# A hybrid encoder step on one core: parameter loads and transposes at the head, the last rotation of the convolution, and every second high part of its normed frames moved

## The chip, the cores and the metric

One Trainium2 chip, one of its cores. The metric is the device time of one execution in microseconds (us), the median of three runs. The engines are called PE (TensorE), DVE (VectorE), ACT (ScalarE), POOL (GpSimd) and SP (SyncE, which only issues transfers here).

## The reference

One inference step over 512 prompt frames and 32 sample frames of width 1024, with two layers. Layer 0 has chunk-band attention and gated linear attention side by side, layer 1 a Conformer convolution module. Each is followed by a squared-ReLU MLP of width 4096. The part that the change touches:

```python
def conv_module(xn, buf, w1, b1, w_dw, b_dw, ln_g, ln_b, w2, b2):
    u = xn @ w1 + b1
    u = u[..., :D_MODEL] * jax.nn.sigmoid(u[..., D_MODEL:])
    full = jnp.concatenate([buf.astype(u.dtype), u], axis=1)
    y = lax.conv_general_dilated(full, w_dw.astype(full.dtype)[:, None, :], window_strides=(1,),
                                 padding='VALID', dimension_numbers=('NWC', 'WIO', 'NWC'),
                                 feature_group_count=D_MODEL) + b_dw
    y = jax.nn.silu(layer_norm(y, ln_g, ln_b))
    return y @ w2 + b2, full[:, -(CONV_W - 1):]
```

## The kernel before, in words

All 544 frames stay in SBUF, channels on partitions: `resid` holds 8 tiles of 128 channels x 544 frames. Every weight matrix is streamed in units of 1024 x 256 (1 MB); there are 92. SP loads a unit into one of two buffers `w_raw` (L416) as soon as the buffer's last user has been split. ACT makes its high part (`split_hi`, L608, type fp32r), DVE its low part (`split_lo`, L1514), and PE multiplies: high x high, high weights x low frames, low weights x high frames, 48 products a tile of 128 output channels (`tile`, L1017; `together` L1040 takes both tiles of a unit column by column, `by_halves` L1056 does so for half of the frames at a time). Frames come as a high part `x_h` and a low part `x_l` too. The order of work on each engine is written out by hand and tied by semaphores: an engine executes its list in order and waits where its next instruction needs another's.

The head: SP loads the rows of x, two weight units and then 23 small parameter loads (`load_parameters`, L386). PE transposes x into four rotating slots of PSUM (L996), which DVE copies to `resid` (L1568); ACT and DVE make high and low parts (L637, L1536). PE runs unit 0 (`together`, with the wait `x_ready` per column), then transposes the parameters (`parameters`, L1077 to L1085), then runs unit 1. DVE scales unit 0's result (L1609, which frees its slot in PSUM) and then copies the parameters (L1579 to L1591).

Before long pauses PE runs dummy products (`keep_clock`, L980) on `ones`.

Between the first MLP and the convolution module comes a norm (`norm`, ACT L643 and L676, DVE L1551 and L1557), then ACT's split of the module's second weight unit, then the first gate (sigmoid, L894).

The convolution: 8 column tiles `m`. Unit `m` of `c_w_pw1` gives gate and value; DVE multiplies them into `glu` (L1912). PE does 20 to 24 of the 31 taps as 32 x 32 diagonal products (`taps`, L1398) and needs for them three copies of the tile whose partitions are rotated by 32, 64 and 96, `glu_rot`. POOL makes them: six transfers per column (L579, L580), counted in `moved`. DVE does the rest of the taps (L1929 to L1936) and the sample frames (L1948), then adds PE's sums (L1961, which waits for `taps_done`). After the last column come the layer norm over channels: means by PE (`add_mean`, L1414), DVE subtracts (L1990), ACT squares (L934), PE sums (L1438), ACT takes the root (L927), DVE inverts (L1994).

Then the normed frames, 16 pieces `j` (8 column tiles for the first 288 frames, 8 for the other 256): DVE scales by 1/std (`cv_scaled`, L2001), ACT applies Silu (L944) into one of three tiles `xn`, ACT copies it to `x_h` (L947), DVE subtracts for `x_l` (L2011), and PE multiplies it by the first unit of `c_w_pw2` (`by_halves`, L1056). DVE's list is: low part of `j`, scaling of `j + 2`, and so on, with the low part of the next weight unit behind `j = 3` (L1514).

Of the kernel before, what the change touches and what calls it, by code (L numbers as in the profile page):

```python
# [74 lines left out]
def tile0(u):  # L75


    return 8 + 2 * u
# [6 lines left out]
def hybrid_kernel(nc, x_prompt, x_sample, cache_a_k, cache_a_v, state_b, cache_c, norm_mix_g, norm_ffn_g,  # L85
# [160 lines left out]
    gains_T, gains_ready = sem("gains_T"), sem("gains_ready")  # L246
    r_ready, x_sums, r_rows, r_spread, r_T = (
        sem(n) for n in ("r_ready", "x_sums", "r_rows", "r_spread", "r_T"))

    x_copied = [sem(f"x_copied{n}") for n in range(4)]  # L250
# [129 lines left out]
    def _(sp):  # L380
# [5 lines left out]
        def load_parameters():  # L386
            for at, n, src in ((V_B1, 16, as_rows(c_b_pw1)), (V_BDW, 8, as_rows(c_b_dw)), (V_LNG, 8, as_rows(c_ln_g)),
                               (V_LNB, 8, as_rows(c_ln_b)), (V_B2, 8, as_rows(c_b_pw2)), (V_GB, 2, as_rows(b_gate_b)),
                               (V_ON, 1, b_out_norm_g)):
                sp.dma_start(vec_rows[at:at + n, :], src).then_inc(rows_landed, 16)  # L390
            for at, src in ((V_QG, a_q_norm_g), (V_KG, a_k_norm_g)):
                for b in range(2):
                    sp.dma_start(vec_rows[at:at + 1, b * DA:(b + 1) * DA], src).then_inc(rows_landed, 16)
            sp.dma_start(wlr[:], w_view(w_in_ab[0])[:, :, N_PROJ * P:N_PROJ * P + RANK]).then_inc(rows_landed, 16)
# [7 lines left out]
            sp.dma_start(gate_w[:], b_gate_w_up[0]).then_inc(rows_landed, 16)  # L402
            sp.dma_start(rel, a_rel_bias[0]).then_inc(rows_landed, 16)
            sp.dma_start(state_s[:], state_b[0, 0].rearrange("(a b) k v -> (b k) a v", b=2)).then_inc(rows_landed, 16)
# [30 lines left out]
        stream(U_PW2, 4, columns(c_w_pw2[0]))  # L435
# [13 lines left out]
    def _(pool):  # L449
# [123 lines left out]
        for m in range(KT):  # L573
# [16 lines left out]
    def _(act):  # L590
# [7 lines left out]
        for at, src in ((V_MIX, norm_mix_g), (V_FFN, norm_ffn_g)):  # L598
            act.dma_start(vec_rows[at:at + 16, :], as_rows(src)).then_inc(gains_landed, 16)

# [54 lines left out]
        for k in range(KT):  # L655
            hi_gain(0, x_h, k, V_MIX, x_copied[k % 4], k // 4 + 1)
            if k == 1:
                split_hi(0, 0, 0)
                for late in (6, 7):
                    act.wait_ge(gemm_done, late + 1)  # L660
                    act.activation(resid[:, late, :], flat(late % 4)[:, 0:TOK], ACT.Copy).then_inc(x_copied[late % 4], 1)
# [1417 lines left out]
```

## Time and profile before

| what | value |
|---|---|
| median of 3 runs | 1371.54 us (1370.0 to 1373.36) |
| the profiled execution | 1374.85 us, of which the span of its core 1373.1 us |
| granted clock of PE, mean | 0.993 of full speed |
| PE busy | 1344.9 us (98%) |
| PE weight loads | 1274.7 us (93%), beside the products |
| DVE busy | 703.2 us (51%) |
| ACT busy | 472.7 us (34%) |
| POOL busy | 86.5 us (6%) |
| chain of waits, by engine | PE 90%; DVE 5%; ACT 2%; issue 2%; DMA 1% |
| chain of waits, the line of `tile` | 70% |
| moved by DMA | 119.90 MB, mean 87 GB/s |

The span is the time from the first to the last instruction of the profiled execution, whose own time is a little longer. Busy shares are means over the whole span; what a change in one stage does is read from that stage.

### The profile page before, as it was taken

Reading aid. Unit: us, or ns where it says so; the run is one execution under the profiler, and the core shown is the slowest. Engines: PE = TensorE matmul, PEld = TensorE weight load, DVE = VectorE, ACT = ScalarE, POOL = GpSimd, SP = SyncE. Lnnn points to the kernel's source line nnn. Section 1 sums busy time; section 2 is a strip of 40 time slices with the busy share of each in tenths; the row PEclk is TensorE's granted clock in tenths of the full one; section 3 lists DMA queues with packets and bytes.
Section 4 is the critical chain, followed back from the end, with each engine's and each line's share of the span. In section 5 each row is a group of like instructions: output and inputs, shape, how many; then the busy total and the mean of one; then the engine's idle time right before and its main releaser. Section 6 shows DMA issues by size and latency. Waiting matters only on the chain.

```text
span 1373.1 us, 27650 instructions
## 1 busy us (share of the span) xinstructions
PE 1344.9 (98%) x11649; PEld 1274.7 (93%) x11649; DVE 703.2 (51%) x1028; ACT 472.7 (34%) x792; POOL 86.5 (6%) x145
## 2 busy tenths in 40 slices
PE   8999999999999999999999999989999999999998
PEld 7998888779999999999999888858999999999998
DVE  5693568575544334334324788877544334334322
ACT  4221556434333223123122544445433223223111
POOL 4001100001100000000011111101100000000000
PEclk9999999999999999999999999999999999999999
DMA  7223300222222222222221433302222221222221
GB/s 253 80 92 106 119 27 2 95 72 93 82 83 82 92 92 92 92 85 74 96 84 62 112 110 106 104 16 69 93 93 92 93 92 61 95 90 92 92 78 50
DMA packets 107293, 119.90 MB, mean 87 GB/s; under 512 B 4435, under 2 KB 103358, under 8 KB 106943
## 3 DMA queue, kind: packets, MB, share of 16 engines
q1 hardware_dynamic: 102783, 101.50, 23.1%
q0 software_dynamic: 4352, 17.02, 4.2%
q8 instruction: 72, 1.18, 0.3%
q14 instruction: 22, 0.18, 0.0%
q10 hardware_dynamic: 64, 0.02, 0.0%
HBM read 104.66 MB, written 7.21 MB: 81 GB/s over the span
## 4 chain that ended last, share of the span: by engine, by line
PE 90%; DVE 5%; ACT 2%; issue 2%; DMA 1%; POOL 0%; SPq 0%; DVEq 0%; ACTq 0%; POOLq 0%
PE ps L1017 70%; PE ps L1173 4%; PE ps L1398 3%; PE ps L1040 3%; DVE rstd L1613 2%; PE ps L1190 1%; PE ps L1284 1%; PE ps L980 1%; PE ps L1223 1%; PE ps L1207 1%; PE ps L1056 1%; PE ps L1002 1%; DVE w_l L1514 1%; PE ps L1438 1%; DMA x_rows<-in_x_sample 1%
## 5 line engine op out<-in xcount | busy, mean ns | idle before, releaser
L608 ACT ACTIVATE w_h<-w_raw 128x2048 fp32r<-128x2048 f32 x92 | 175.4, 1907 | 276.4 <-PE ps L1017 272.9
L1514 DVE TENSOR_TENSOR w_l<-w_raw,w_h 128x2048 fp32r<-128x2048 f32 x92 | 210.8, 2291 | 102.8 <-ACT w_h L608 102.7
L1017 PE MATMUL ps<-x_h,w_h 128*128 128x272 f32 x1152 | 242.0, 292 | 2.4 <-ACT sig L894 1.5
L1017 PE MATMUL ps<-x_l,w_h 128*128 128x272 f32 x1152 | 238.6, 288 | 0.0
L1017 PE MATMUL ps<-x_h,w_l 128*128 128x272 f32 x1152 | 238.2, 288 | 0.0
L1017 PE MATMUL ps<-xf_h,w_h 128*128 128x272 f32 x1024 | 212.9, 289 | 0.0
L1017 PE MATMUL ps<-xf_l,w_h 128*128 128x272 f32 x1024 | 211.2, 287 | 0.0
L1017 PE MATMUL ps<-xf_h,w_l 128*128 128x272 f32 x1024 | 210.9, 287 | 0.0
L1017 PEld LDWEIGHTS ps<-x_h,w_h 128*128 128x128 f32 x1152 | 180.9, 189 | 9.1 <-issue 8.7
L1017 PEld LDWEIGHTS ps<-x_l,w_h 128*128 128x128 f32 x1152 | 182.6, 189 | 0.0
L1017 PEld LDWEIGHTS ps<-x_h,w_l 128*128 128x128 f32 x1152 | 180.7, 188 | 0.0
L1017 PEld LDWEIGHTS ps<-xf_l,w_h 128*128 128x128 f32 x1024 | 161.5, 188 | 0.0
L1017 PEld LDWEIGHTS ps<-xf_h,w_h 128*128 128x128 f32 x1024 | 159.9, 188 | 0.2
L1017 PEld LDWEIGHTS ps<-xf_h,w_l 128*128 128x128 f32 x1024 | 159.8, 188 | 0.0
L1861 DVE TENSOR_TENSOR resid<-ps,resid 128x544 f32 x64 | 46.3, 724 | 200.6 <-PE ps L1017 199.7
L870 ACT ACTIVATE relu<-relu 128x544 f32<-128x544 f32 x64 | 42.2, 659 | 239.9 <-DVE relu L1879 239.9
L1017 PE MATMUL ps<-odd_h,w_h 128*128 128x272 f32 x512 | 106.8, 290 | 0.0
L1017 PE MATMUL ps<-odd_l,w_h 128*128 128x272 f32 x512 | 105.6, 287 | 0.0
L1017 PE MATMUL ps<-odd_h,w_l 128*128 128x272 f32 x512 | 105.5, 287 | 0.0
L1879 DVE SCALAR_TENSOR_TENSOR relu<-ps,xn 128x544 f32<-128x544 f32 x64 | 46.2, 722 | 89.6 <-PE ps L1017 89.5
L1017 PEld LDWEIGHTS ps<-odd_l,w_h 128*128 128x128 f32 x512 | 80.8, 188 | 0.0
L1017 PEld LDWEIGHTS ps<-odd_h,w_l 128*128 128x128 f32 x512 | 79.9, 188 | 0.0
(278 smaller groups left out, 1653.5 us busy)
## 6 DMA issues: line engine op xcount, KB each, us to landing
w_raw<-in_w_ffn_up SPq DMA_DIRECT2D x32, 1024.0 KB, 5.3
w_raw<-in_w_ffn_down SPq DMA_DIRECT2D x32, 1024.0 KB, 5.1
w_raw<-in_w_in_ab SPq DMA_DIRECT2D x12, 1024.0 KB, 5.3
w_raw<-in_c_w_pw SPq DMA_DIRECT2D x12, 1024.0 KB, 6.1
w_raw<-in_w_out_ab SPq DMA_DIRECT2D x4, 1024.0 KB, 5.5
glu_rot<-glu POOLq DMA_DIRECT2D x16, 203.2 KB, 5.4
resid_scratch<-resid POOLq DMA_DIRECT2D x1, 2176.0 KB, 8.1
resid<-resid_scratch POOLq DMA_DIRECT2D x1, 2176.0 KB, 9.0
```

Of the source, the lines that this page charges most:

```text
L608: act.activation(w_h[s][:], w_raw[:, s], ACT.Copy).then_inc(w_hi, 1)
L870: act.activation(relu2[:, m, :], relu[:, m, :], ACT.Square).then_inc(relu2_done, 1)
L980: pe.matmul(ps[:, bank, 0:2 * P], any_bits[:, 0:P], any_bits, start=True, stop=True)
L1002: ins = pe.matmul(dst[:, a, :], w[:], src[:, a * n:(a + 1) * n], start=start, stop=stop)
L1017: ins = pe.matmul(ps[:, 2 * m + t, 0:HALF], a[s][:, k, w], b[:, k, t * HALF:(t + 1) * HALF], start=(k == 0 and q == 0), stop=(k == KT - 1 ...
L1040: ins = pe.matmul(ps[:, 2 * m + t, 0:HALF], a[s][:, k, w], b[:, k, t * HALF:(t + 1) * HALF], start=(k == 0 and q == 0), stop=(k == KT - 1 ...
L1173: ins = pe.matmul(ps[:, 2 * m + t, 0:HALF], a[u % 2][:, k, m * P:(m + 1) * P], b[:, k, t * HALF:(t + 1) * HALF], start=(k == 0 and q == 0) ...
L1398: ins = pe.matmul(ps[to, 4 + r, :], diag[rows, s, tap, :], src, start=(n == 0), stop=(n == rounds(m) - 1))
L1514: dve.tensor_tensor(w_l[s][:], w_raw[:, s], w_h[s][:].bitcast(F32), ALU.subtract).then_inc(w_lo, 1)
L1613: dve.reciprocal(rstd[:, 0:TOK], sumsq[:]).then_inc(rstd_ready, 1)
L1861: dve.tensor_tensor(r, slot(m), r, ALU.add).then_inc(slot_free[m], 1)
L1879: dve.scalar_tensor_tensor(out=halves(relu[:, m, :]), in0=slot(m), scalar=0.0, in1=halves(r_tok), op0=ALU.max, op1=ALU.mult).then_inc(slot ...
```

## The change

It moves work, and changes nothing that is computed. (1) Of the parameter loads eleven go from SP's list to ACT's; the eight that PE's transposes need stay on SP, ahead of the second weight unit, and four follow it with a semaphore of their own, `late_rows`. (2) x is transposed into three slots instead of four, PE transposes the parameters ahead of unit 0 and runs eight dummies behind them, and DVE copies the parameters before it scales. (3) ACT splits the second unit of `c_w_pw1` ahead of the second norm. (4) Of the last column's six rotations the three that end at partition 128 go to ACT's queue, counted in `moved_last`; SP holds the third unit of `c_w_pw2` until all six have landed; PE runs eight dummies ahead of the last taps. (5) POOL copies every second `x_h` of the normed frames.

```diff
-    x_copied = [sem(f"x_copied{n}") for n in range(4)]
+    x_copied = [sem(f"x_copied{n}") for n in range(3)]
...
             if first:
                 for s in range(2):
                     sp.dma_start(w_raw[:, s], source(s)).then_inc(w_landed[s], 16)
-                load_parameters()
+                    (load_parameters, load_late_parameters)[s]()
...
-        stream(U_PW2, 4, columns(c_w_pw2[0]))
+        stream(U_PW2, 2, columns(c_w_pw2[0]))
+
+        sp.wait_ge(moved[(KT - 1) % 2], KT // 2 * 96 - 48)
+        sp.wait_ge(moved_last, 48)
+        stream(U_PW2 + 2, 2, columns(c_w_pw2[0], 512))
...
                 pool.dma_start(glu_rot[0:at, m % 2, j - 1, :], glu[P - at:P, m, 0:PAD + SEQ]).then_inc(moved[m % 2], 16)
-                pool.dma_start(glu_rot[at:P, m % 2, j - 1, :], glu[0:P - at, m, 0:PAD + SEQ]).then_inc(moved[m % 2], 16)
+                if m < KT - 1:
+                    pool.dma_start(glu_rot[at:P, m % 2, j - 1, :], glu[0:P - at, m, 0:PAD + SEQ])\
+                        .then_inc(moved[m % 2], 16)
+
+
+        for j in range(1, 2 * KT, 2):
+            c, k = j // KT, j % KT
+            pool.wait_ge(cv_silu, j + 1)
+            pool.tensor_copy(x_h[:, k, cv_span(c)], xn[:, j % 3, cv_span(c)]).then_inc(cv_hi_odd, 1)
...
         ffn(0, U_FFN0, lambda u: phase(u, 4, squares_of(2, u)))
+        split_hi(U_PW1, 0, 1)
         norm(2, X_MIX1)
...
-        split_hi(U_PW1, 0, 1)
...
         split_hi(U_PW2, 0, 1)
+
+        act.wait_ge(slot_free[1], KT - 1 + (tile0(U_PW1) // 2 + 1))
+        act.wait_ge(taps_done, KT)
+        for j in range(1, ROTS):
+            at = P - j * (P // ROTS)
+            act.dma_start(glu_rot[at:P, (KT - 1) % 2, j - 1, :], glu[0:P - at, KT - 1, 0:PAD + SEQ])\
+                .then_inc(moved_last, 16)
         act.activation(no_use[:], eps[:], ACT.Sqrt)
...
-            act.wait_ge(cv_silu, j + 1)
-            act.activation(x_h[:, k, cv_span(c)], xn[:, j % 3, cv_span(c)], ACT.Copy).then_inc(cv_hi, 1)
+            if j % 2 == 0:
+                act.wait_ge(cv_silu, j + 1)
+                act.activation(x_h[:, k, cv_span(c)], xn[:, j % 3, cv_span(c)], ACT.Copy).then_inc(cv_hi, 1)
...
-            pe.wait_ge(rows_landed, 16 * 23)
+            pe.wait_ge(rows_landed, 16 * 19)
...
-        for n in range(4):
-            pe.wait_ge(x_copied[n], 2)
+        parameters()
+        for n in range(2):
+            pe.wait_ge(x_copied[n], 3)
+        keep_clock(8, 0)
         together(0, 0, x_h, x_l, x_ready)
-        parameters()
...
+        pe.wait_ge(slot_free[1], tile0(U_PW2) // 2)
+        keep_clock(8, 2)
         taps(KT - 1)
...
             if u == 0:
+                parameters()
                 dve.wait_ge(r_ready, 1)
...
-            if u == 0:
-                parameters()
...
-            dve.wait_ge(cv_hi, j + 1)
+            dve.wait_ge((cv_hi, cv_hi_odd)[j % 2], j // 2 + 1)
```

PE at the head, from the last transpose of x to the first products of unit 0. Before:

```order
L996 MATMUL ps<-ident,x_rows 128x128 x4
L996 MATMUL ps<-ident,x_rows 128x32
L1040 MATMUL ps<-x_h,w_h 128x272 x2
L1040 MATMUL ps<-x_l,w_h 128x272 x2
L1040 MATMUL ps<-x_h,w_l 128x272 x2
```

Now:

```order
L1021 MATMUL ps<-ident,x_rows 128x128 x4
L1021 MATMUL ps<-ident,x_rows 128x32
L1102 MATMUL ps<-ident,vec_rows 128x85
L1104 MATMUL ps<-ident,dw_rows 128x31 x8
L1107 MATMUL ps<-ident,dw_cross 128x18 x8
L1110 MATMUL ps<-ident,cc_rows 128x30 x8
L1005 MATMUL ps<-ones 128x256 x8
L1065 MATMUL ps<-x_h,w_h 128x272 x2
```

The 25 transposes of parameters and eight dummies have come between the transposes of x and unit 0.

SP's queue at the head, which has to bring those parameters. Now (before, both weight units stood ahead of all small loads):

```order
L387 DMA x_rows<-in_x_sample 32x1024
L408 DMA w_raw<-in_w_in_ab 128x8x256
L390 DMA dw_rows<-in_c_w_dw 31x1024
L394 DMA dw_cross<-in_c_w_dw 6x8x96
L395 DMA dw_cross<-in_c_w_dw 6x8x32
L394 DMA dw_cross<-in_c_w_dw 6x8x64
L395 DMA dw_cross<-in_c_w_dw 6x8x64
L394 DMA dw_cross<-in_c_w_dw 6x8x32
L395 DMA dw_cross<-in_c_w_dw 6x8x96
L396 DMA cc_rows<-in_cache_c 30x1024
L408 DMA w_raw<-in_w_in_ab 128x8x256
L399 DMA wlr<-in_w_in_ab 128x8x16
```

The second weight unit has moved behind eight loads, and four stand behind it.

ACT at the normed frames behind the convolution, the first pieces. Before:

```order
L944 ACTIVATE xn<-cv,vecs 128x288
L947 ACTIVATE x_h<-xn 128x288
L944 ACTIVATE xn<-cv,vecs 128x288
L947 ACTIVATE x_h<-xn 128x288
L944 ACTIVATE xn<-cv,vecs 128x288
L947 ACTIVATE x_h<-xn 128x288
```

Now:

```order
L968 ACTIVATE xn<-cv,vecs 128x288
L972 ACTIVATE x_h<-xn 128x288
L968 ACTIVATE xn<-cv,vecs 128x288 x2
L972 ACTIVATE x_h<-xn 128x288
L968 ACTIVATE xn<-cv,vecs 128x288 x2
L972 ACTIVATE x_h<-xn 128x288
```

Every second copy has left ACT's list; POOL's has eight of them, between its last rotations and the store of the convolution's cache.

## Rows read from the trace of the kernel before

**Rows 1.** timeline of PE, head of the kernel (start us, us, engine, line, operation, idle before)
```profile
18.25 0.61 PE L1040 MATMUL ps<-x_h,w_h 128*128 128x272 f32 x2 [2.28 <-DVE x_l L1536]
...
32.74 0.24 PE L1077 MATMUL ps<-ident,vec_rows 85*128 85x85 f32 x1
...
34.51 0.52 PE L1017 MATMUL ps<-x_h,w_h 128*128 128x272 f32 x2
```
**Rows 2.** busy time and granted clock of one stretch at the head
```profile
18.25:21.90 3.65, 3.65 (x17) 3.65 (x18) 3.33 (x5) 3.62 (x7) 0.00 (x0) 0.53 0.22 69
```
**Rows 3.** timeline of DVE, after the first unit's product
```profile
32.25 1.41 DVE L1609 TENSOR_TENSOR proj<-ps,xn 128x544 f32<-128x544 f32 x2 [4.76 <-PE ps L1040]
```
**Rows 4.** timeline of SP's queue, parameter loads
```profile
3.50 1.21 SPq L410 DMA_DIRECT2D w_raw<-in_w_in_ab  x2
4.74 5.57 SPq L390 DMA_DIRECT2D vec_rows<-in_c_b_pw  x1
...
13.97 0.43 SPq L395 DMA_DIRECT2D dw_rows<-in_c_w_dw  x1
...
19.25 0.46 SPq L401 DMA_DIRECT2D cc_rows<-in_cache_c  x1
```
**Rows 5.** landing times of the first two weight tiles (L410)
```profile
DMA to landing us min/median/max: 9.6/10.8/12.0
```
**Rows 6.** the page's costliest groups: ACT's split (x count, busy, mean ns)
```profile
L608 ACT ACTIVATE w_h<-w_raw 128x2048 fp32r<-128x2048 f32 x92 | 175.4, 1907 | 276.4 <-PE ps L1017 272.9
```
**Rows 7.** timeline of ACT, second norm and first gate
```profile
744.68 0.71 ACT L643 ACTIVATE sumsq<-ps,eps 128x544 f32<-128x544 f32 x1 [2.69 <-PE ps L1002]
...
763.12 1.28 ACT L894 ACT_TABLE_LOAD   x1 [2.01 <-PE ps L1040]
```
**Rows 8.** timeline of PE, end of the convolution
```profile
889.22 4.15 PE L1414 MATMUL ps<-cv,mean_d 128*128 128x288 f32 x16
...
897.45 1.08 PE L1398 MATMUL ps<-glu,diag 32*32 32x512 f32 x4 [4.08 <-DMA glu_rot<-glu]
...
910.68 1.04 PE L980 MATMUL ps<-ones 128*128 128x256 bf16 x8
```
**Rows 9.** timeline of DVE, end of the convolution
```profile
906.35 0.69 DVE L1961 TENSOR_TENSOR rstd<-ps,rstd 128x512 f32<-128x512 f32 x1 [7.04 <-PE ps L1398]
```
**Rows 10.** busy time and granted clock, last column's taps
```profile
897.40:902.30 4.90, 4.85 (x90) 2.17 (x97) 1.84 (x3) 0.00 (x0) 0.00 (x0) 0.50 0.00 0
```
**Rows 11.** timeline of POOL, last rotations
```profile
887.98 0.52 POOL L579 DMA_DIRECT2D glu_rot<-glu  x1 [14.62 <-DVE glu L1912]
```
**Rows 12.** DMA issues of 764 to 777 us (KB each, us to landing)
```profile
glu_rot<-glu POOLq DMA_DIRECT2D x2, 203.2 KB, 3.6
```
**Rows 13.** DMA issues of 884 to 899 us
```profile
glu_rot<-glu POOLq DMA_DIRECT2D x2, 203.2 KB, 5.9
```
**Rows 14.** timeline of DVE, normed frames behind the convolution
```profile
926.28 2.29 DVE L1514 TENSOR_TENSOR w_l<-w_raw,w_h 128x2048 fp32r<-128x2048 f32 x1
...
932.46 0.43 DVE L2011 TENSOR_TENSOR x_l<-xn,x_h 128x256 fp32r<-128x256 f32 x1
...
932.80 0.49 DVE L2001 TENSOR_TENSOR xn<-cv,rstd 128x224 f32<-128x224 f32 x2
...
934.41 0.43 DVE L2011 TENSOR_TENSOR x_l<-xn,x_h 128x256 fp32r<-128x256 f32 x1
```
**Rows 15.** timeline of ACT, normed frames behind the convolution
```profile
933.33 0.60 ACT L944 ACTIVATE xn<-xn,vecs 128x256 f32<-128x256 f32 x1
...
933.96 0.42 ACT L947 ACTIVATE x_h<-xn 128x256 fp32r<-128x256 f32 x1
```
**Rows 16.** timeline of 946.7 to 949 us, DVE and POOL
```profile
946.78 2.27 DVE L1514 TENSOR_TENSOR w_l<-w_raw,w_h 128x2048 fp32r<-128x2048 f32 x1
...
948.16 1.39 POOL L475 COPY sumsq<-sq 128x544 f32<-128x544 f32 x1
```
**Rows 17.** POOL's copy of a frame tile (ns min/median/max)
```profile
L475 POOL COPY sumsq<-sq x3: 633/639/1393, 318.0 to 948.2; 128x544 f32<-128x544 f32 x3
```

More of the change, by code:

```diff
@@ L246, in hybrid_kernel @@
     gains_T, gains_ready = sem("gains_T"), sem("gains_ready")
+    moved_last = sem("moved_last")
+    cv_hi_odd = sem("cv_hi_odd")
+    late_rows = sem("late_rows")
     r_ready, x_sums, r_rows, r_spread, r_T = (
         sem(n) for n in ("r_ready", "x_sums", "r_rows", "r_spread", "r_T"))
-    x_copied = [sem(f"x_copied{n}") for n in range(4)]
+    x_copied = [sem(f"x_copied{n}") for n in range(3)]
     vec_T = sem("vec_T")
@@ L386, in load_parameters @@
         def load_parameters():
[L387 to L394, printed above, removed]
             sp.dma_start(dw_rows[:], c_w_dw[0]).then_inc(rows_landed, 16)
@@ L401, in load_parameters, with load_late_parameters @@
             sp.dma_start(cc_rows[:], cache_c[0, 0]).then_inc(rows_landed, 16)
-            sp.dma_start(gate_w[:], b_gate_w_up[0]).then_inc(rows_landed, 16)
-            sp.dma_start(rel, a_rel_bias[0]).then_inc(rows_landed, 16)
-            sp.dma_start(state_s[:], state_b[0, 0].rearrange("(a b) k v -> (b k) a v", b=2)).then_inc(rows_landed, 16)
+        def load_late_parameters():
+            sp.dma_start(wlr[:], w_view(w_in_ab[0])[:, :, N_PROJ * P:N_PROJ * P + RANK]).then_inc(late_rows, 16)
+            sp.dma_start(gate_w[:], b_gate_w_up[0]).then_inc(late_rows, 16)
+            sp.dma_start(rel, a_rel_bias[0]).then_inc(late_rows, 16)
+            sp.dma_start(state_s[:], state_b[0, 0].rearrange("(a b) k v -> (b k) a v", b=2)).then_inc(late_rows, 16)
         def stream(u0, units, source, first=False):
@@ L599, in _ @@
             act.dma_start(vec_rows[at:at + 16, :], as_rows(src)).then_inc(gains_landed, 16)
+        for at, n, src in ((V_B1, 16, as_rows(c_b_pw1)), (V_BDW, 8, as_rows(c_b_dw)), (V_LNG, 8, as_rows(c_ln_g)),
+                           (V_LNB, 8, as_rows(c_ln_b)), (V_B2, 8, as_rows(c_b_pw2)), (V_GB, 2, as_rows(b_gate_b)),
+                           (V_ON, 1, b_out_norm_g)):
+            act.dma_start(vec_rows[at:at + n, :], src).then_inc(rows_landed, 16)
+        for at, src in ((V_QG, a_q_norm_g), (V_KG, a_k_norm_g)):
+            for b in range(2):
+                act.dma_start(vec_rows[at:at + 1, b * DA:(b + 1) * DA], src).then_inc(rows_landed, 16)
         def split_hi(u, i, d):
@@ L655, in _ @@
         for k in range(KT):
-            hi_gain(0, x_h, k, V_MIX, x_copied[k % 4], k // 4 + 1)
+            hi_gain(0, x_h, k, V_MIX, x_copied[k % 3], k // 3 + 1)
             if k == 1:
@@ L660, in _ @@
                     act.wait_ge(gemm_done, late + 1)
-                    act.activation(resid[:, late, :], flat(late % 4)[:, 0:TOK], ACT.Copy).then_inc(x_copied[late % 4], 1)
-                    act.wait_ge(x_copied[late % 4], 2)
+                    act.activation(resid[:, late, :], flat(late % 3)[:, 0:TOK], ACT.Copy).then_inc(x_copied[late % 3], 1)
+                    act.wait_ge(x_copied[late % 3], 3)
         for n, c in enumerate((3, 4)):
@@ L988, in _ @@
         for k in range(KT):
-            if k >= 4:
-                pe.wait_ge(x_copied[k % 4], 1)
+            if k >= 3:
+                pe.wait_ge(x_copied[k % 3], k // 3)
             for c in range(TT + 1):
@@ L995, in _ @@
                 M = width(c)
[L996 removed]
+                ins = pe.transpose(flat(k % 3)[:, c * P:c * P + M], x_rows[0:M, c, k * P:(k + 1) * P],
                                    ident[0:M, 0:M])
@@ L1133, in x_ready @@
             if k == KT - 2:
+                pe.wait_ge(x_copied[2], 2)
                 pe.wait_ge(r_spread, 1)
@@ L1387, in taps @@
             pe.wait_ge(slot_free[1], m + (tile0(U_PW1) // 2 + 1))
-            pe.wait_ge(moved[s], (m // 2 + 1) * 96)
+            if m < KT - 1:
+                pe.wait_ge(moved[s], (m // 2 + 1) * 96)
+            else:
+                pe.wait_ge(moved[s], (m // 2 + 1) * 96 - 48)
+                pe.wait_ge(moved_last, 48)
             if m:
@@ L1585, in parameters @@
             dve.wait_ge(vec_T, 3)
+            dve.wait_ge(late_rows, 16 * 4)
             dve.tensor_copy(cc_T[:].rearrange("p k c -> p (k c)"), ps[:, 6, 0:KT * PAD]).then_inc(vec_ready, 1)
```

5 lines of the change are left out of this document (2 added, 3 removed).

## The prediction

> **What bounds the kernel now.** I read the page first: TensorE (PE) is busy almost throughout and carries nine tenths of the chain of waits. So I cut nothing from the long runs of weight units; only stretches where PE stands still, runs at the lower of its two clocks (1.2 instead of 2.4 GHz), or is fed more slowly than it computes can change. The list of PE's waits and the granted clock then name three such places that the change touches. Durations come from one execution of 1374.85 us; the median of the runs is 1371.54 us, 3.3 us below. I work out a difference in the time base of that execution and take it off the median. About 0.3%, 4.1 us, is what a measurement of this kernel can tell from no change.
>
> Place one, the head. PE has finished its transposes of x at 15.97 us and stands for 2.28 us until the first low part is there; then it runs 3.65 us at a granted clock of 0.53 [rows 1, 2]. At 32.74 it does the parameter transposes, until unit 1 begins at 34.51 [rows 1]. Place two, the end of the convolution: PE's column means end at 893.37, then it waits 4.08 us for the last rotated copy of glu, and the taps run 4.9 us at a clock of 0.50; DVE, done with its own taps at 906.35 - 7.04 = 899.31, stands 7.04 us for them [rows 8, 9, 10]. Place three, the normed frames behind the convolution: DVE and ACT hand each column to and fro, and PE takes what they deliver [rows 14, 15].
>
> **The head.** The 25 transposes of parameters move from behind unit 0 into PE's idle 2.28 us. They took 34.51 - 32.74 = 1.77 us, so they end at 17.74; eight dummies follow, 1.04 us as the eight at 910.68 [rows 1, 8], so the product can start at about 18.8 instead of 18.25: +0.55. With no pause before it I take the higher clock throughout; the 3.65 us at 0.53 become 3.65 x 0.53 = 1.93: -1.7. The 1.77 behind unit 0 go: -1.77. What is late next is a slot in PSUM: unit 1 now follows at once, and DVE needs until it has scaled the first half of unit 0 (two such in 1.41 us, 0.7 each [rows 3]), of which about 0.3 stand out behind the product: +0.3. Before, the transposes hid that. DVE's own parameter copies move ahead of the scaling into its idle 4.76 us [rows 3] and cost nothing; without that cover they would hold the scaling up. Sum of the head: 0.55 - 1.7 - 1.77 + 0.3 = **-2.6**. It ends no worse than about 0 (rival b), and at best at -2.9, where the slot costs nothing.
>
> It hangs on the data. On SP's queue eight parameter loads now stand ahead of the second weight tile. Their issue took from 13.97 to 19.71, 5.7 us [rows 4]. The two weight tiles were issued from 3.50 on, by 4.7 both [rows 4]. Issued from 4.0 on the eight loads end at 9.8; the first weight tile, ahead of them in the queue, lands at 3.5 + 9.6 = 13.1 [rows 5], so I expect them by 14 to 15, and PE wants them at 15.97. The second weight tile landed 12.0 behind its issue, near 16.0 [rows 5]; issued at 9.8 it lands about there still, for it had to wait for the bytes ahead of it anyway, and ACT splits it only behind its row squares, which come after all of x's high parts. The eleven small loads of vec_rows move to ACT's queue, where ACT has nothing to do until x is transposed; the four late ones follow the second tile, and DVE's wait on them sits where it is idle anyway. Three slots for the transposes instead of four: a slot is wanted again three column tiles later, and DVE, which copies each while PE makes the next, is never more than one behind, so 0. If the loads come late, PE stands (rival b). The rest of the projection waits link by link on this point, so I let the 2.6 through to the end.
>
> **The split ahead of the second norm.** ACT's split of a weight tile, 1.9 us [rows 6], moves to where ACT idles 2.69 us before the root at 744.68 [rows 7]: cover enough, by 0.8. Behind the norm PE waits not for the split but for ACT's sigmoid, whose table load starts only at 763.12, when unit 0 is done [rows 7]. So 0.
>
> **The last rotation.** Of its six transfers three stay with POOL and three go to ACT's queue. POOL began at 887.98 and needs 0.52 an issue [rows 11]: six end at 891.1, three at 889.5. And SP now holds the next weight tile (1 MB) until both have landed. With that tile in the same microseconds a large rotation took 5.9 us to land [rows 13]; at the first column, where the tile was well ahead, 3.6 [rows 12]. I take 3.6: last landing 889.0 + 3.6 = 892.6, before the means end at 893.37. Ends of the range: 889.0 + 5.9 = 894.9, or nothing gained (897.4). The eight dummies (1.04) then lead to taps at 894.4 instead of 897.45, and 4.9 us at 0.50 become 2.45: the taps took 906.35 - 897.45 = 8.9, now 6.45, end 900.85. DVE's own taps end at 899.31 [rows 9], still before; that cover is 1.4 us, and it is what would be late next. So **-5.5**. The held tile is wanted only when the next unit but one is split, behind place three, so it costs 0. ACT's three issues and its table load fall before the squares, where ACT waits for the same taps; 0.
>
> A rule speaks against this split. The Trainium skill, "DMA: Bandwidth & Descriptors", section "Issuing engines are not separate DMA queues", says that transfers started by several engines share the same 16 DMA engines, and that issuing them side by side saves only the issue time. By that rule alone, without the held tile, the saving is three issues of 0.52, and the step would be worth some 4 us; that is rival c.
>
> **Every second high part on GpSimd (POOL).** Per column: DVE scales, ACT applies Silu, ACT copies the high part, DVE subtracts the low part; DVE scales column j+2 only behind the low part of j. From low part to low part, two columns on: 0.34 to the scaling, 0.49 for its two pieces, Silu 933.33 to 933.93, copy 933.96 to 934.38, low part at 934.41: 934.41 - 932.46 = 1.95, with no slack anywhere [rows 14, 15]. ACT's own load per pair, two Silus and two copies, is as long: 2 x (0.60 + 0.42) = 2.0, a little of it overlapped. So relieving ACT alone shortens nothing: the loop does. The even columns' loop stays at 1.95. In the odd one POOL's copy takes ACT's place. POOL copied 544 columns in 0.63; under DVE's subtraction of two SBUF tiles it took 1.39, until 949.55 [rows 16, 17]: its 0.63 began at 948.9, as DVE ended at 949.05. I read that as POOL shut out while DVE reads two tiles. In this loop all of DVE's operations read two, four of them per pair (0.34 + 0.49, twice, 1.66 [rows 14]). Add POOL's copy, 0.4 by its columns, and a hand-over, and a pair takes about 2.2 instead of 1.95. Four pairs of the second half: +1.0. The first half: +0.4 before DVE's weight split at 926.28, and +0.6 behind it, since the copy of column 5 is shut out for the split's 2.29 us and then holds DVE up. Sum **+2.0**; the bounds are -1.2 (ACT was the bound, and four pairs fall by 0.3 to DVE's 1.66) and +5 (the copy writes another type than those rows, at 0.4 more each on 8 copies).
>
> The Trainium skill, "SBUF — State Buffer", section "Who interferes with whom", has it that a VectorE instruction with two SBUF inputs contends with a GpSimd instruction that reads SBUF, one waiting for the other in full, and that ScalarE never waits. By that rule the sum is the +2.0 above, and with neither engine ever shut out -1.2; the row of 1.39 agrees with the rule, though it is one row.
>
> **Sum.** -2.6 + 0 - 5.5 + 2.0 = **-6.1 us**, so 1371.54 - 6.1 = **1365.4 us**. Own range -4.2 to -8.2.
>
> **The rivals.**
> (a) ACT's queue was the bound of place three and POOL relieves it. For it: ACT is busy nearly throughout there. Against: the loop of 1.95 without slack. -2.6 - 5.5 - 1.2 = -9.3: **1362.2**. Chance 0.10.
> (b) The parameters land late. The first parameter load stood 5.57 us in SP's queue behind two weight tiles [rows 4]; should it stand as long behind one, the last is issued at 15.4 and lands near 18, PE runs transposes and dummies to 20.8, on a cooled clock that they warm again: the head comes to about 0 and the sum to -3.5, **1368.0**. Against: the second tile itself was taken without a stall. Chance 0.10.
> (c) The rotations land only as much earlier as three issues of 0.52 take, at 895.7 instead of 897.2: taps of 6.45 end at 902.15, DVE resumes 4.2 earlier: -2.6 - 4.2 + 2.0 = -4.8, **1366.7**. Chance 0.10. If they don't land earlier at all, the step does not do what it says: -0.6, **1370.9**, chance 0.04.
> (d) POOL's converting copy is dear, 0.4 to 0.5 above a plain one: +3 to +4 on top: about -2.6, **1368.9**. Chance 0.11.
> (e) Slower: POOL's copy with its shutting-out takes so long that it sets place three alone. Each odd column is in the loop, so each microsecond above my 0.4 costs 8 us in all. The gain is eaten at 0.4 + 6.1/8 = 1.2 us a copy; at 2.0 (nearest row 1.39 for twice the columns [rows 16]) the sum is -6.1 + 8 x 1.6 = +6.7: **1378.2**. Chance 0.05.
> The forecast keeps 0.50.
>
> **How the numbers follow.** Faster by over 0.3% (below 1367.4): the forecast 0.50, (a) 0.10, (c) 0.10, together 0.70. Within 0.3%: (b) 0.10, (d) 0.11, the empty rotation 0.04, together 0.25. Slower: 0.05. The range runs from 1362.0, which holds (a), to 1369.8, past (d); outside lie (e), the empty rotation and the tails.
>
> **What would show it.** Head: granted clock 1.0 from 18 us on, unit 1 at about 31.9 instead of 34.51. Convolution: no wait on glu_rot before the last taps, DVE's idle before its first partial sum 1.4 us or so instead of 7.04. Place three: POOL copies above 0.4 us where DVE works, DVE idle before its low parts put down to POOL, a pair at 2.2. A PE wait of microseconds before the parameter transposes, or POOL copies past 1.2 us, would make the forecast wrong.

## The result and the profile after

| | time, median | range | to the kernel before (95% interval) |
|---|---|---|---|
| before | 1372.3 us (10 runs) | 1370.0 to 1373.36 | |
| after | 1375.2 us (10 runs) | 1372.18 to 1376.4 | 1.0024 (1.0015 to 1.0032) |

The change made the kernel 2.9 us slower by the medians, where I had forecast 6.1 us faster. The profiled execution took 1375.81 us with a span of 1374.1, against 1374.85 and 1373.1 before. So in the traces the difference is only +1.0. I set the two traces side by side, instruction by instruction, and read where their distance changes, that is, by how much later (+) the changed kernel comes to the same instruction. It changes for good in three places and nowhere else by more than 0.2 us.

| place | distance ahead | distance behind | this place | forecast |
|---|---|---|---|---|
| head (to the second unit's scaling) | 0 | +5.0 to +5.1 | **+5.1** | -2.6 |
| last rotation and taps (to DVE's first partial sum) | +5.3 | -0.23 | **-5.5** | -5.5 |
| normed frames (to the last low part) | -0.23 | +0.94 | **+1.2** | +2.0 |

**The head.** PE's timeline, in the columns of [rows 1]:

```profile
11.14 5.56 PE L1021 MATMUL ps<-ident,x_rows 32*128 32x32 f32 x36
20.26 0.40 PE L1102 MATMUL ps<-ident,vec_rows 85*128 85x85 f32 x1 [3.56 <-DMA cc_rows<-in_cache_c]
...
23.29 1.89 PE L1005 MATMUL ps<-ones 128*128 128x256 bf16 x8
24.83 0.80 PE L1065 MATMUL ps<-x_h,w_h 128*128 128x272 f32 x2
...
39.56 0.49 PE L1042 MATMUL ps<-x_h,w_h 128*128 128x272 f32 x2 [0.65 <-DVE proj L1643]
```

PE stands 3.56 us for the parameter loads. The row names cc_rows, the last of them to be issued on SP; all nineteen count on one semaphore, so which of them landed last the row can't tell. Unit 0 starts at 24.83 and not at 18.25 or at my 18.8; unit 1 at 39.56 instead of 34.51. Transposes and dummies take 24.83 - 20.26 = 4.57 us instead of 2.81, since the clock has fallen in the wait, and it is still down as the product starts. SP's queue, and the same wait in the chain of waits:

```profile
3.90 0.61 SPq L390 DMA_DIRECT2D dw_rows<-in_c_w_dw  x1
...
10.44 0.70 SPq L396 DMA_DIRECT2D cc_rows<-in_cache_c  x1
11.18 1.75 SPq L408 DMA_DIRECT2D w_raw<-in_w_in_ab  x1
```

```profile
10.44 9.79 DMA cc_rows<-in_cache_c
```

Busy time in two stretches (granted clock, DMA share and GB/s are the last three numbers):

```profile
24.90:26.80 1.90, 1.90 (x11) 1.90 (x10) 1.90 (x2) 0.87 (x1) 1.01 (x2) 0.50 0.37 129
17.50:19.00 1.50, 0.00 (x0) 0.00 (x0) 1.50 (x3) 1.50 (x3) 0.00 (x0) 1.00 0.07 22
```

The eight loads were issued by 11.1, where I had 9.8. But the last landed at 20.2, not at 14 to 15, and 1.3 us of issue don't make up for that. The second row says how: while PE waits, the 16 DMA engines are busy for 0.07 of their time and move 22 GB/s. That is the work of about one engine (0.07 x 16 = 1.1). Many bytes in the way are not what PE waits for. The second weight tile, too, landed only 11.3 us behind its issue, at 22.5, where I had it near 16; nothing waited for it.

**The end of the convolution.** PE, DVE and SP, then the busy time of the 4.9 us that [rows 10] show for the kernel before:

```profile
898.52 1.04 PE L1005 MATMUL ps<-ones 128*128 128x256 bf16 x8
899.51 0.63 PE L1429 MATMUL ps<-glu,diag 32*32 32x512 f32 x4
```

```profile
906.12 0.69 DVE L1994 TENSOR_TENSOR rstd<-ps,rstd 128x512 f32<-128x512 f32 x1 [1.49 <-PE ps L1429]
```

```profile
899.42 0.37 SPq L414 DMA_DIRECT2D w_raw<-in_c_w_pw  x1
```

```profile
899.40:904.30 4.90, 4.90 (x156) 3.02 (x166) 4.87 (x6) 0.00 (x0) 0.00 (x0) 1.00 0.64 217
```

No wait on glu_rot is left, the clock is 1.0 instead of 0.50, and DVE's idle time is 1.49 us instead of 7.04 [rows 8 to 10]. SP, which now waits for the same landing, resumes at 899.42: just as PE's dummies end. Of the last rotation's issues (KB each, us to landing), two rows:

```profile
glu_rot<-glu POOLq DMA_DIRECT2D x1, 203.2 KB, 3.1
glu_rot<-glu ACTq DMA_DIRECT2D x1, 203.2 KB, 4.9
```

**The normed frames.** DVE, the answer to [rows 14]:

```profile
926.22 2.29 DVE L1547 TENSOR_TENSOR w_l<-w_raw,w_h 128x2048 fp32r<-128x2048 f32 x1
928.42 0.68 DVE L2044 TENSOR_TENSOR x_l<-xn,x_h 128x288 fp32r<-128x288 f32 x1
...
933.20 0.69 DVE L2034 TENSOR_TENSOR xn<-cv,rstd 128x224 f32<-128x224 f32 x2
933.87 0.42 DVE L2044 TENSOR_TENSOR x_l<-xn,x_h 128x256 fp32r<-128x256 f32 x1
934.22 0.49 DVE L2034 TENSOR_TENSOR xn<-cv,rstd 128x224 f32<-128x224 f32 x2
...
936.02 0.42 DVE L2044 TENSOR_TENSOR x_l<-xn,x_h 128x256 fp32r<-128x256 f32 x1
```

and two of POOL's eight copies:

```profile
927.03 1.76 POOL L590 CAST x_h<-xn 128x288 fp32r<-128x288 f32 x1 [1.59 <-ACT xn L968]
...
933.38 0.46 POOL L590 CAST x_h<-xn 128x256 fp32r<-128x256 f32 x1 [1.68 <-ACT xn L968]
```

A pair of columns takes 936.02 - 933.87 = 2.15 us, before 1.95. POOL's copy that is released under DVE's weight split takes 1.76 and ends 0.3 behind it. While the copy of 933.38 runs, DVE's scaling takes 0.69 instead of 0.49. So in these rows each is once the one that is held up.

### The profile page after: what moved, and what is told of

It is laid out like the page before. It is cut to its first block, busy times and chain, and to the rows that moved or that the text cites. A ratio compares the mean times of both kernels' runs of the same rounds, so it can differ in the third digit from the quotient of the medians.

```text
span 1374.1 us, 27674 instructions
## 1 busy us (share of the span) xinstructions
PE 1347.6 (98%) x11665; PEld 1276.1 (93%) x11665; DVE 703.8 (51%) x1028; ACT 469.4 (34%) x784; POOL 89.6 (7%) x150
## 4 chain that ended last, share of the span: by engine, by line
PE 90%; DVE 5%; ACT 2%; issue 1%; DMA 1%; SPq 1%; POOL 0%; ACTq 0%; DVEq 0%; POOLq 0%
PE ps L1042 71%; PE ps L1200 4%; PE ps L1429 3%; PE ps L1065 3%; DVE rstd L1647 2%; PE ps L1005 1%; PE ps L1217 1%; PE ps L1311 1%; PE ps L1250 1%; PE ps L1234 1%; PE ps L1027 1%; DMA cc_rows<-in_cache_c 1%; DVE w_l L1547 1%; PE ps L1471 1%; PE ps L1138 0%
```

## The experiments

Twelve kernels ran, in three sets of four, each set beside its own runs of the kernel before. Their medians of before were 1370.7, 1371.7 and 1372.4 us, so the ratios are what to compare. The intervals are 3 to 4 us wide.

| kernel | median us | ratio to before (95% interval) |
|---|---|---|
| e_head: the head's part alone | 1377.81 | 1.0047 (1.0032 to 1.0062) |
| e_tail: all but the head | 1370.28 | 0.9993 (0.9983 to 1.0003) |
| e_rot: e_tail without POOL's copies | 1368.65 | 0.9982 (0.9971 to 0.9993) |
| e_nocross: change, dw_cross late | 1373.36 | 1.0013 (1.0002 to 1.0024) |
| e_split: change, loads in pieces of 16 rows and the rest | 1370.20 | 0.9996 (0.9982 to 1.0011) |
| e_nodw: e_nocross, dw_rows late too | 1367.98 | 0.9977 (0.9962 to 0.9993) |
| e_dummies: e_rot and twelve dummies | 1366.80 | 0.9973 (0.9959 to 0.9988) |
| e_again: before, unchanged | 1373.51 | 1.0015 (1.0000 to 1.0030) |
| e_nohold: e_rot, weight tile not held | 1372.08 | 1.0002 (0.9992 to 1.0012) |
| e_pool6: e_rot, all rotations on POOL | 1368.69 | 0.9977 (0.9966 to 0.9989) |
| e_best | 1367.69 | 0.9966 (0.9954 to 0.9978) |
| e_best_more | 1365.87 | 0.9952 (0.9936 to 0.9968) |

### The parts by themselves: e_head, e_tail, e_rot

e_head takes all parts of the diff that touch the loads, x_copied and the parameters. e_tail takes the others. e_rot is e_tail with this taken back:

```diff
-        for j in range(1, 2 * KT, 2):
-            c, k = j // KT, j % KT
-            pool.wait_ge(cv_silu, j + 1)
-            pool.tensor_copy(x_h[:, k, cv_span(c)], xn[:, j % 3, cv_span(c)]).then_inc(cv_hi_odd, 1)
-            if j % 2 == 0:
-                act.wait_ge(cv_silu, j + 1)
-                act.activation(x_h[:, k, cv_span(c)], xn[:, j % 3, cv_span(c)], ACT.Copy).then_inc(cv_hi, 1)
+            act.wait_ge(cv_silu, j + 1)
+            act.activation(x_h[:, k, cv_span(c)], xn[:, j % 3, cv_span(c)], ACT.Copy).then_inc(cv_hi, 1)
```

> The kernel before with the change's parts behind the second norm alone (the weight split ahead of it, the last rotation, every second high part on POOL); the head as it was. Theory A (the parts stand by themselves: head +5.1, rotation -5.35, POOL's copies +1.2, as the two traces have them): 4.1 us faster than before, unit 1 at 34.5 as before. Theory B (the gain at the rotation is only there because the head moved everything, or is eaten further on): within 1 us of before.

> As the run before it, but ACT makes all the high parts of the normed frames again: only the split and the last rotation are changed. Theory A: 5.3 us faster than before, 1.2 us faster than with POOL's copies. If POOL's copies relieve ACT after all, it is slower than the run with them.

> The kernel before with the head's part alone (loads reordered, three slots, parameter transposes and eight dummies ahead of unit 0). Theory A: 5.1 us slower than before, PE waiting 3.6 us for cc_rows until 20.2. If the profiled execution of the change was unlucky in its head (its first dummies ran at half the pace, 0.75 us), some 4.3 us slower. By the forecast's own sum it would be 2.6 us faster.

For the head theory A holds: alone it costs 0.0047 x 1371 = 6.4 us (4.4 to 8.5), and its trace has PE wait 4.72 us for the parameters, until 20.93. For the rest the times don't decide. e_tail came out 1.0 us faster, with an interval that holds 0, where A had 4.1 and B "within 1 us"; its profiled head also ran slow, with unit 1 at 37.40 and not at 34.5. e_rot, without POOL's copies, is 2.5 us faster, clear of 0 but under half of A's 5.3. The two parts add up to 1.0040, the change has 1.0024; the intervals cover the gap. What speaks for A are the sizes in the traces, which repeat. From DVE's first partial sum to the last low part e_rot takes 933.10 - 900.13 = 32.97 us, as before (939.31 - 906.35 = 32.96), and e_tail 937.88 - 903.74 = 34.14. So POOL's copies cost **1.2 us**, and a pair of columns in e_rot is back at 1.95:

```profile
927.25 0.42 DVE L2034 TENSOR_TENSOR x_l<-xn,x_h 128x256 fp32r<-128x256 f32 x1 [0.16 <-ACT x_h L964]
...
929.20 0.42 DVE L2034 TENSOR_TENSOR x_l<-xn,x_h 128x256 fp32r<-128x256 f32 x1 [0.16 <-ACT x_h L964]
```

By ratio POOL's copies cost 1.5 us (e_tail beside e_rot), with intervals that overlap. One thing doesn't fit: the rotation is worth 5.5 us in the traces of the change and of e_rot, but only 2.5 by the ratio of times (interval 1.0 to 4.0). I come back to it.

### What makes the parameters late: e_nocross, e_nodw, e_split

My first theory was that the six small loads of dw_cross occupied the one engine. In e_nocross they go behind the second weight tile, with a semaphore of their own; their eight transposes follow unit 0:

```diff
         def load_late_parameters():
+            for j in range(1, ROTS):
...
+                sp.dma_start(to[:, :, 0:ROTS - j, :], of[:, :, j:ROTS, :]).then_inc(late_rows, 16)
+                sp.dma_start(to[:, :, ROTS - j:ROTS, :], of[:, :, 0:j, :]).then_inc(late_rows, 16)
...
         together(0, 0, x_h, x_l, x_ready)
+        cross_parameters()
```

> The changed kernel, with the six loads of dw_cross taken out of the batch that PE waits for: they go behind the second weight tile, and their eight transposes go behind unit 0. Theory C (the six loads of small pieces occupy one or two DMA engines for some 7 us, and cc_rows, behind them on those engines, lands only when they are through): cc_rows lands at 13 to 15, PE's wait before the parameter transposes is gone, unit 1 starts at 32 to 33 instead of 39.6, the kernel is 6 us or more faster than the change. Theory D (the parameters are late because they stand behind 3 MB of x and weights on one queue, whatever they are): they land at 18 to 20 still and the time is within 1 us of the change.

Both theories fell. PE in e_nocross, and busy time, clock and DMA of the stretch before that row:

```profile
19.24 0.29 PE L1103 MATMUL ps<-ident,vec_rows 85*128 85x85 f32 x1 [2.67 <-DMA vec_rows<-in_a_k_norm_g]
```

```profile
16.00:19.20 3.20, 0.56 (x5) 0.29 (x3) 3.20 (x3) 2.97 (x5) 0.00 (x0) 1.00 0.13 37
```

PE's wait still ended at 19.24, one microsecond earlier: so not dw_cross (C). Yet by 15.5 nearly all bytes of x and of both weight tiles had moved, the second tile's too, which stands behind the parameters (287 GB/s over 15.5 us are 4.4 MB; x and the two tiles are 4.3), and from 16 to 19.2 the DMA share was 0.13: so not the bytes in front either (D). (The second tile's last part landed at 4.71 + 17.3 = 22.0, later than the parameters. That fits one engine that is behind all others; no run was made for it.) By time e_nocross is 1.5 us faster than the change by ratio, with intervals that overlap. What was left was the time from the first weight tile's landing (3.17 + 10.4 = 13.6) to the parameters' (19.2): 5.6 us. That is what the 124 KB of dw_rows take at the 22 to 25 GB/s of one engine (5.1 to 5.8). dw_rows has 31 rows. That is theory E; the next two kernels were made for it. e_nodw moves dw_rows, too, behind the second weight tile, and its transposes behind unit 0:

```diff
-            sp.dma_start(dw_rows[:], c_w_dw[0]).then_inc(rows_landed, 16)
...
         def load_late_parameters():
+            sp.dma_start(dw_rows[:], c_w_dw[0]).then_inc(late_rows, 16)
```

e_split leaves everything in the changed kernel's order and only cuts the loads:

```diff
-            sp.dma_start(dw_rows[:], c_w_dw[0]).then_inc(rows_landed, 16)
+            for a, b in ((0, 16), (16, CONV)):
+                sp.dma_start(dw_rows[a:b], c_w_dw[0, a:b]).then_inc(rows_landed, 16)
...
-            sp.dma_start(cc_rows[:], cache_c[0, 0]).then_inc(rows_landed, 16)
+            for a, b in ((0, 16), (16, PAD)):
+                sp.dma_start(cc_rows[a:b], cache_c[0, 0, a:b]).then_inc(rows_landed, 16)
```

> The changed kernel with dw_rows (31 rows) and cc_rows (30 rows) each loaded in two pieces, 16 rows and the rest. Theory E (a load whose rows don't divide by 16 goes through one DMA engine: 124 KB at the 25 GB/s or so that the tail of the loads shows take 5 us, behind that engine's share of x and of the weight tile, which landed at 13.1 to 13.6): the pieces of 16 rows spread, the rest is half as long, PE's wait for the parameters ends at 16.5 to 18 instead of 20.2, and the kernel is 2.5 to 3.5 us faster than the change. Theory D (whatever is in that queue lands at 19 to 20): the wait ends at 19 or later, within 1 us of the change.

> As the run with dw_cross taken out of the early batch, and dw_rows taken out too: PE's early wait is for the eleven vec_rows on ACT's queue and cc_rows alone, in the same places of the queues. Theory E, with dw_rows the one that occupies an engine: wait gone or under 1 us (rows landed by 17), unit 0 starts at 18.5 to 19.5, 2 us or more faster than with dw_rows in the batch. If cc_rows is as slow (30 rows don't divide by 16 either) it ends at 18 to 19 still. If ACT's queue is what is late (vec_rows issued at 5.7 landed 13.5 later by the trace), it ends at 19 still.

PE's timeline in e_split, then in e_nodw:

```profile
16.04 0.29 PE L1104 MATMUL ps<-ident,vec_rows 85*128 85x85 f32 x1
...
19.11 0.67 PE L1067 MATMUL ps<-x_h,w_h 128*128 128x272 f32 x2 [0.20 <-DVE x_l L1571]
```

```profile
16.45 0.29 PE L1103 MATMUL ps<-ident,vec_rows 85*128 85x85 f32 x1
...
19.27 0.49 PE L1066 MATMUL ps<-x_h,w_h 128*128 128x272 f32 x2 [0.82 <-DVE x_l L1575]
```

The wait is gone in both: the transposes of parameters follow those of x at once. The same bytes in the same place of the queue, only in two loads each, land by 16.0 instead of 20.2. And the one-engine tail, in e_nodw (dw_rows whole, late) and in e_split:

```profile
18.50:20.00 1.50, 0.73 (x6) 0.77 (x7) 1.50 (x3) 1.50 (x4) 0.00 (x0) 1.00 0.06 25
```

```profile
18.50:19.50 1.00, 0.80 (x6) 0.54 (x5) 1.00 (x2) 1.00 (x3) 0.00 (x0) 0.88 0.01 3
```

A share of 0.06 is one engine of 16. With dw_rows cut it is gone. cc_rows whole (30 rows) was no trouble in e_nodw, nor were the 15 rows left over in e_split; so my "doesn't divide by 16" was too wide. It is 31 that goes through one engine.

The Trainium skill has the rule that my sum lacked: "DMA: Bandwidth & Descriptors", section "Why a DMA increments its semaphore by 16 and not by 1", says that a copy is spread over the largest number of engines, up to 16, that divides its slowest dimension. By it 31 rows get one engine, 30 and 15 rows fifteen, 16 rows sixteen. The traces agree as far as they go: a stretch at one engine's share with 31 rows, none seen with 30, 16 or 15; how many engines those used no run here shows.

e_nodw also clears ACT's queue, which the row of e_nocross names: its eleven loads stand in the same places there and had landed by 16.45.

By the ratios e_split is 3.8 us faster than the change (1.0024 - 0.9996) and e_nodw 6.4; both still have POOL's copies. The step that moves dw_rows alone, from e_nocross to e_nodw, is 0.0036 x 1371 = 4.9 us, with intervals that don't touch. e_split gave about what was expected; its profiled head still lost some of it: the clock fell to 0.50 at 19.5, right behind the start of unit 0, with no wait longer than 0.2 us ahead. Why it fell there I can't say.

### What the rotation's gain rests on: e_nohold, e_pool6

The change moved half of the last rotation to ACT's queue and held SP's next weight tile. e_nohold takes the second away, e_pool6 the first:

```diff
 e_nohold
-        stream(U_PW2, 2, columns(c_w_pw2[0]))
-        sp.wait_ge(moved[(KT - 1) % 2], KT // 2 * 96 - 48)
-        sp.wait_ge(moved_last, 48)
-        stream(U_PW2 + 2, 2, columns(c_w_pw2[0], 512))
+        stream(U_PW2, 4, columns(c_w_pw2[0]))
 e_pool6
-            act.dma_start(glu_rot[at:P, (KT - 1) % 2, j - 1, :], glu[0:P - at, KT - 1, 0:PAD + SEQ])\
-                .then_inc(moved_last, 16)
+                pool.dma_start(glu_rot[at:P, m % 2, j - 1, :], glu[0:P - at, m, 0:PAD + SEQ])\
+                    .then_inc(moved[m % 2] if m < KT - 1 else moved_last, 16)
```

> As the run with the split and the rotation alone, but SP loads the next weight tile when it is free, as before; three rotations on POOL's queue and three on ACT's. If the issue time alone mattered (forecast's rival c), the last landing moves by 1.5 us only with or without the hold: PE still waits about 2.5 us for glu_rot. If sharing the DMA engines with the 1 MB tile is what made the landing 5.9 us, all of the gain beyond those 1.5 us needs the hold: PE waits 1.5 to 3 us, DVE's idle before its partial sum is 4 to 6 us instead of 1.5, and the time is 2 to 4 us above the run with the hold.

> As the run with the split and the rotation alone, but all six transfers of the last rotation stay on POOL's queue; SP's tile is held until they have landed. If the hold does most of it: last issue ends at POOL's start + 3.1, landing 3 to 3.6 behind that, at +6.5 of POOL's start, about where ACT's transfers land in the change (+6.1): PE's wait is under 0.7 us and the time within 1 us of that run. If the second queue is what counts, PE waits 1.5 us or more.

e_nohold, PE's timeline and two of its issues:

```profile
896.48 0.90 PE L1415 MATMUL ps<-glu,diag 32*32 32x512 f32 x4 [3.53 <-DMA glu_rot<-glu]
```

```profile
glu_rot<-glu POOLq DMA_DIRECT2D x1, 203.2 KB, 6.1
glu_rot<-glu ACTq DMA_DIRECT2D x1, 203.2 KB, 8.5
```

and e_pool6, the same:

```profile
893.50 0.63 PE L1412 MATMUL ps<-glu,diag 32*32 32x512 f32 x4 [0.17 <-issue]
```

```profile
glu_rot<-glu POOLq DMA_DIRECT2D x2, 203.2 KB, 3.3
```

Without the hold nothing is left of the gain: 1.0002, a wait of 3.53 us, more than the 1.5 to 3 expected, and DVE idle for 6.62 us. With the hold and one queue it is all there: 0.9977. The second queue is worth nothing here. It shortens the issuing, but the transfers then take longer to land: 3.1 to 4.9 us in the change, 2.9 to 3.7 in e_pool6. Counted from POOL's first issue, SP resumes after 899.42 - 893.29 = 6.1 us in the change and after 893.41 - 887.07 = 6.3 in e_pool6; counted from the first issue on either queue (ACT's, 893.03) the change has 6.4, and nothing is gained. In e_nohold the tile is issued at 885.61 and the rotations from 886.42 on, while its bytes are on their way.

e_nohold's clock falls with its wait, so the pair also shows what the place is worth by medians: 1372.08 - 1368.69 = 3.4 us, where the two traces differ by 4.9 there (e_nohold is 0.4 us ahead of e_pool6 before it and 4.5 behind after it). e_again, the kernel before once more, had the wait as well (3.65 us), but less of it at the lower clock: 0.72 over the six microseconds from 897 on, and DVE idle for 5.83 us, not 7.04. Set beside the first trace of the same kernel it is 1.2 us shorter at this place. So the profile I predicted from had the place at its dearest, and part of the gap between traces and medians is that the clock behind this wait differs between executions; what makes up the rest stays open.

> The kernel before, unchanged. It tells how far two samples of one kernel lie apart, and what a second profiled execution shows of the last taps of the convolution: if the wait of 4.1 us for the rotation and the 4.9 us at half clock behind it are in every execution, both are there again and DVE's idle is 7 us; if they are a matter of chance, the clock there is 1.0 and the idle 4.5 us. Time: as before, within 0.1%.

By time, e_again came out at 1.0015 (1.0000 to 1.0030) against the other runs of the same kernel, more than the 0.1% I had expected. Two kernels that lie within 0.15% here are not told apart, least of all in different sets.

### The clock in the head, and a version that beats both: e_dummies, e_best, e_best_more

e_dummies is e_rot and one line, ahead of unit 0 with the head as before:

```diff
         for n in range(4):
             pe.wait_ge(x_copied[n], 2)
+        keep_clock(12, 0)
```

> The kernel before with the split and the last rotation of the change, ACT making all high parts, the head's loads as before, and only twelve dummies ahead of unit 0 from the head's part. Theory F (the idle 2.28 us ahead of unit 0 cost some executions their clock, and the dummies alone keep it): unit 0 at the higher clock from its start, no start later than 19.2, 1 to 2 us faster by the median than the same kernel without them (1368.7), so about 1367, 3 to 4 us faster than before. Rival: the clock falls at other places of the head as well, by chance, and nothing is gained: 1368.7.

It was 1.9 us faster than e_rot by medians and 1.2 us by ratio, with intervals that overlap: in the right direction, not shown. In its profiled execution unit 0 started at 21.69 and not by 19.2, for another loss, which e_tail's had too. e_tail, PE's timeline:

```profile
10.11 0.33 PE L1019 MATMUL ps<-ident,x_rows 128*128 128x128 f32 x1 [1.19 <-DMA x_rows<-in_x_prompt]
...
10.70 9.27 PE L1019 MATMUL ps<-ident,x_rows 32*128 32x32 f32 x36
```

In eight of the fourteen profiled executions PE makes its second batch of dummies at half pace (3.1 to 3.2 us instead of 1.7) and reaches this tile of x after it has landed; the transposes then take 5.56 us. Where PE is at full pace early, it waits for the tile. In four executions it waited 1.0 to 1.25 us there, and three of these ran the transposes in 8.2 to 9.3 us, at a granted clock of 0.51 to 0.60 from 10.6 to 18.7; none of the ten others did. e_best puts together what had helped: the rotation with its hold, ACT making all high parts, the split loads, dw_rows and dw_cross late. e_best_more covers that wait as well. To e_nodw, e_best adds the cut loads as in e_split and takes POOL's copies back as in e_rot; e_best_more is e_best with one more edit:

```diff
-                    keep_clock((0, 14, 6, 2, 2)[c], 6)
+                    keep_clock((0, 14, 6, 10, 2)[c], 6)
```

> The changed kernel without POOL's high parts (ACT makes them all), with dw_rows and dw_cross behind the second weight tile and their transposes behind unit 0, and with dw_rows and cc_rows loaded as 16 rows and the rest. The sum of what the runs so far show: 1.2 to 1.6 us faster than the run with dw_rows out of the early batch (1368.0), so 1366.5; with the one-engine tail gone perhaps another 0 to 1 us where the third weight tile lands sooner.

> As the run before it, with ten dummies instead of two ahead of the third x tile. Theory G (in four of ten profiled executions PE was early at that tile, waited 1.0 to 1.25 us for it, and in three of these ran its transposes of x in 8.2 to 9.3 us at half clock instead of 5.56): the dummies cover that wait, no profiled head has transposes of over 6 us, and the slow tail of the run's times (clock 0.995 and below) is gone; the median falls by up to 1 us. Against: where PE is late at that tile already (dummies at half pace) the eight more cost 0.65 us each time.

e_best_more's PE timeline:

```profile
9.80 1.25 PE L1002 MATMUL ps<-ones 128*128 128x256 bf16 x10
...
11.31 5.56 PE L1018 MATMUL ps<-ident,x_rows 32*128 32x32 f32 x36
```

Both beat the kernel before and the change: 0.9966 and 0.9952, 4.7 and 6.6 us. e_best came 1.2 us above what I expected by median, 0.5 by ratio. e_best_more's five runs all lie between 1364.04 and 1366.65 and at a clock of 0.998 or 0.999; every other kernel has at least one run at or below 0.994. Its interval overlaps e_best's, and five runs are few: that the extra dummies remove the tail is likely, not shown. Its profiled head was one of the slow-starting kind, in which no wait was to be covered, and paid for them: ten dummies took 1.25 us where two take 0.38, and x's transposes began at 11.31, e_nodw's at 10.96.

## Why the prediction was wrong, step by step

**The head: wrong, -2.6 against +5.1.** The step that failed is "Issued from 4.0 on the eight loads end at 9.8; the first weight tile, ahead of them in the queue, lands at 13.1, so I expect them by 14 to 15". The issues ended at 11.1, the landing was at 20.2. I had taken the queue for one pipe, in which little stands behind the weight tile. It feeds sixteen engines, and the 124 KB of dw_rows stood on one of them, for 5.1 to 5.8 us that my sum had at nothing. Behind the weight tile's 13.1 that makes 18.2 to 18.9; of the rest up to 20.2 e_nocross, without dw_cross in the batch, saves 1.0, and what is left no run takes apart. The same error is in "it lands about there still", of the second weight tile: it landed at 22.5, without a price. The profile of before held the trace of this, unread: dw_rows was issued at 13.97 there too, and nobody waited for it until 32.74. That cover was what the change took away. How the distance from my sum comes about: x's transposes 0.7 later, the wait 3.56, transposes and dummies at half clock 1.76, together the 6.0 by which unit 0 starts behind my 18.8; the rest of the 7.7 (unit 1 at 39.56, not 31.9) is half clock at the start of the product and a slot wait of 0.65 where I had 0.3.

Rival (b), the parameters late, was the right family, with another mechanism (the stall of an issue) and too small: it had them at 18 and the head at zero. With the landing mended the head seems to gain, though not 2.6: in e_best DVE's third scaling comes at 38.99 instead of 40.85, 1.9 us sooner, of which x's earlier transposes are 0.2; sixteen of the 25 parameter transposes stand behind unit 0 there again. And I had taken one profiled head for the head: in e_again, the same kernel as before, that scaling came at 43.69, 2.8 us later, nearly all of it by the clock. In the seven traces with the loads of before it lies between 40.85 and 43.74, in e_nodw, e_best and e_best_more between 38.99 and 39.77. By time (e_best 0.9966 beside e_pool6's 0.9977) the gain is not shown.

**The split ahead of the second norm: right**, 0; the distance of the traces is +5.13 behind the feed-forward units and +5.12 at the first column's partial sums.

**The last rotation: right in size in the trace, -5.5.** Taps at 899.5 are 894.2 in the time base of before (forecast 894.4). One input was off: the last landing was not 3.6 but 4.9 us behind its issue, on ACT's queue, so at 899.3 and not at 897.9 (892.6 + 5.3). The eight dummies hid that. That the number came out to the tenth is in part luck of the execution it was taken from: against e_again's trace the same place gains 4.3. The weighing was right that the hold was what counts, and rival (c), by which the issue time would be worth 1.5 us without it, was too kind: e_nohold kept none. The Trainium skill's sentence in "Issuing engines are not separate DMA queues" of "DMA: Bandwidth & Descriptors" promises that issuing side by side saves the issue time. Here it saved at most 0.2 us of the 1.5. By the unprofiled times the step is worth 2.5 to 3.4 us.

**POOL's high parts: right in sign, oversized, 1.2 against 2.0.** A pair takes 2.15 (I had 2.2), which gives 0.8 of my 1.0 for the second half. The first half cost 0.4 and not 1.0: the copy shut out by the weight split (1.76 us, 927.03 to 928.79) ended only 0.3 behind DVE, as DVE has another column to do first. The mechanism, two SBUF inputs on DVE against a reading POOL, agrees with the rows from both sides: POOL's copy long under DVE, DVE's scaling long under POOL's copy. Rivals (a), (d) and (e) fell with it: no copy took over 0.63 outside the split.

**The sum.** With the traces' own values it is 5.1 + 0.2 (the distance grows so much at the second column's taps) - 5.5 + 1.2 = +1.0, the distance of the profiled executions. The medians say +2.9. They credit the rotation with less than the traces, of which the execution of before explains 1.2 us; the rest is open. The answer "slower" needed rival (b) at its measured price; I had given slower 0.05 and let it hang on POOL alone.

## What to carry to other kernels

When a load is moved to where something waits for it, look at how its shape divides over the DMA engines and not only at its bytes and its place in the queue: 31 rows kept the parameters 5.6 us behind the weight tile ahead of them, and the same rows as 16 and 15 no time that was seen. A low DMA share (0.06 to 0.07) while an engine waits for a landing is the sign of it. When a transfer lands late, hold back the large one that runs beside it before spreading its issues over queues.

## What the runs showed of the hardware

- A load of 31 rows of 4 KB moved at one DMA engine's share, 25 GB/s at 0.06; with 30, 16 or 15 rows no such stretch was seen. A 1 MB load issued behind it landed after 11.3 us, behind the same rows in two loads after 6.0.
- The last column's six rotations of 68 to 203 KB: on one queue a transfer landed after 5.1 to 6.7 us beside a 1 MB load and after 2.9 to 3.7 without it; on two queues after 6.1 to 8.5 and 3.1 to 4.9.
- DVE's scaling took 0.69 instead of 0.49 while a POOL copy ran, and POOL's copy 1.76 instead of 0.43 to 0.63 under DVE's 2.29 us subtraction.
- PE's clock in the head differed between executions of one kernel: waits of 1.0 to 1.25 us ahead of a busy stretch were followed by a clock of 0.50 in three cases of four, and in e_split it fell without one. Between 92 and 150 us, where nothing was changed, the clock falls for 3.4 or 6.8 us in thirteen of fourteen traces and not at all in e_nodw's; the longer fall cost the trace of before about 1.5 us more than the shorter one cost e_again's.
